# A hybrid decoder step on one core: the sample caches' compressed branch in single-pass matmuls, with its start-up loads and page table rearranged

## The chip, the cores and the metric

The kernel runs on 1 core of one Trainium2 chip. The metric is the device time of one execution in microseconds (us), the median of several runs. Engines are TensorE (PE; its weight loads are PEld), VectorE (DVE), ScalarE (ACT), GpSimd (POOL) and SyncE (SP, which here issues DMAs only).

## What is computed

One inference step of a decoder layer for a prompt of 512 tokens and 8 sample tokens, each sample with 1024 past positions in a paged cache. The change touches only the compressed branch of the samples' attention, and the code just before and behind it. From the reference:

```
def compress_kv(kv, pe, w1, b1, w2, b2):      # kv: cached K/V rows, 8 samples x 1024 positions
    ...
    seg = kv[:, :n_seg * CMP_STRIDE].reshape(B, n_seg, CMP_STRIDE, 2, N_KV, HEAD_DIM)
    w1r = w1.reshape(2, CMP_R, CMP_STRIDE, HEAD_DIM, CMP_HIDDEN)
    proj = jnp.einsum('bsjcgd,crjdf->bsrcgf', seg, w1r)
    hid = sum(proj[:, r:r + n_cmp, r] for r in range(CMP_R))
    pe_term = jnp.einsum('cld,cldf->cf', pe, w1)
    hid = jax.nn.silu(hid + (pe_term + b1)[None, None, :, None, :])
    return jnp.einsum('bncgf,cfd->bncgd', hid, w2) + b2[None, None, :, None, :]
```

Stride 16, blocks of 32, 4 KV heads of 64, hidden 128; c is K or V, r is the half of the block. A page of the cache holds 128 positions, and the page table says which page. Behind this come the norm of x, the input projection, the three attention branches, the SSD heads, the output projection and the MLP, all in float32 accuracy. Large products take three passes over operands split in a high part (type FP32R, written by ScalarE) and a low part (the rest, by VectorE): high x high, high x low, low x high.

## The kernel before

Each engine has one program, a list of functions called in order, and they meet through semaphores. Order of the functions at the start:

- SP: `const_sp`, `x_sp`, `proj_sp`. POOL: `const_pool`, `compress_pool`, `const2_pool`. ACT: `compress_act`, `x_act`, `proj_act`. DVE: `const_dve`, `compress_dve`, `x_dve`, `proj_dve`. PE: `const_pe`, `compress_pe`, `x_pe`, `proj_pe`.

**Start.** `const_sp` issues 12 loads of 128 single words (the page table, repeated onto 128 partitions), then 16 small loads, the last two (`dskip`) of 4-byte words, and after the first gather has landed the weights `w1` (2 MB). `const_dve` turns the table into row indices `idx_c` (4 steps of the branch) and `idx_s`. `compress_pool` gathers 4 MB of cache rows per step by an indirect DMA into the one buffer `seg_raw`; the gather of the next step waits until `seg_raw` has been reordered.

**The branch.** There are N_ST = 4 steps t of 2 samples. In each step DVE copies `seg_raw` into `seg_ord` in 8 pieces (L464, one for each c and KV head), PE turns each piece by 8 transposes of 128x128 into PSUM banks 0 to 3 (`turn`, L368), and ACT and DVE, half of the banks each, copy the turned data to `segT` (L424, L456). Then `products` (L382) does 32 matmuls of 128x512 in plain float32; the trace has each of these as two matmul records, so 64 records in a step. ACT evicts the second half r = 1, DVE adds r = 0 (L479), ACT applies SiLU, and `second_layer` (L390, L397) multiplies by `w2`. `outputs` on DVE (L446, L451) stores the results. PE's order is turn(0), the bias product L331 (64 matmul records with one column each, `w1` as weights), turn(1), products(0), turn(2), second_layer(0), products(1), and so on.

**Behind it.** `x_sp` loads x (4 MB, `xtok`) onto the place of `segT` when products(2) is done, and then `proj_sp` fills the ring `w_raw` of four 0.5 MB weight pieces. `x_pe` turns x, ACT and DVE split it into `h_hi` and `h_lo` (L502, L526), and `proj_act` and `proj_dve` split the weight pieces (`hi_piece` L591, `lo_piece` L597) for the three-pass products of `mul_piece` (L610), which also do the rest of the projections and the MLP.

Of the kernel before, what the change touches and what calls it, by code (L numbers as in the profile page):

```python
# [105 lines left out]
def build_program(nc, i, o):  # L106
    with ExitStack() as ctx:
# [69 lines left out]
        segT = at("segT", [P, 2, 8, 8, P], A2)  # L177
        w1 = at("w1", [P, 2, 2, 8, CHID], A2 + 65536)

        xtok = at("xtok", [P, 4, D_MODEL], A2)  # L180
        xs_tok = at("xs_tok", [NB, D_MODEL], M_LO)
# [22 lines left out]
        ptab_c = at("ptab_c", [P, 4], 11488, I32)  # L204
        ptab_s = at("ptab_s", [P, NB], 11520, I32)
# [26 lines left out]
        SMALL_LOADS.append((pe_row[:], i["cmp_pe"].rearrange("a c (l j) d -> (a c l) (j d)", j=2)))  # L232
# [9 lines left out]
        def const_sp(e):  # L242

            pg = i["page_table"]
            for s in range(4):
                e.dma_start(ptab_c[:, s:s + 1], bass.AP(pg.tensor, 16 * s, [[1, 16], [0, 8]]),
                            allow_slow_non_contiguous=True).then_inc(tab_ld, 16)
            for b in range(NB):
                e.dma_start(ptab_s[:, b:b + 1], bass.AP(pg.tensor, 8 * b, [[1, 8], [0, 16]]),
                            allow_slow_non_contiguous=True).then_inc(tab_ld, 16)  # L250
            e.wait_ge(pool_c, 1)
            for dst, src in SMALL_LOADS:
                e.dma_start(dst, src, allow_slow_non_contiguous=True).then_inc(small_ld, 16)
            e.wait_ge(seg_ld, 16)
            e.dma_start(w1[:].rearrange("p c r j f -> p c (r j) f"),
                        i["cmp_w1"].rearrange("a c (l j) d f -> (a j d) c l f", j=2)).then_inc(w1_ld, 16)

        def const_pool(e, ch):
# [5 lines left out]
            ch.step(e.iota(pidx[:, 0:1], pattern=[[0, 1]], base=0, channel_multiplier=1))  # L264
            ch.step(e.memset(ident[:], 0.0))
            keep(ident[:], ALU.not_equal, 1.0, 0, 1, [[-1, P]])
            ch.settle()
            e.memset(ones[:], 1.0).then_inc(pool_c, 1)

        def const2_pool(e, ch):  # L270
# [4 lines left out]
            for tile, v in ((cmask, 0.0), (causT, 1.0), (cmpmask, 0.0), (same_grp, 1.0), (sel_mat, 1.0),  # L275
                            (sel_m2, 1.0), (own_batch, 1.0), (valid0, 1.0), (small, 1.0), (eps_col, EPS)):
                ch.step(e.memset(tile[:], v))
# [19 lines left out]
        def const_dve(e, ch):  # L297
# [5 lines left out]
            e.wait_ge(tab_ld, 16 * 12)  # L303
            for s in range(4):
                e.scalar_tensor_tensor(out=idx_c[:, s:s + 1], in0=ptab_c[:, s:s + 1], scalar=8.0,
                                       in1=pidx[:, 1:2], op0=ALU.mult, op1=ALU.add).then_inc(idx_rdy, 1)
            for b in range(NB):
                e.scalar_tensor_tensor(out=idx_s[:, b:b + 1], in0=ptab_s[:, b:b + 1], scalar=16.0,
                                       in1=pidx[:, 2:3], op0=ALU.mult, op1=ALU.add).then_inc(idx_rdy, 1)

            e.wait_ge(pe_par, 2)
            ch.step(e.tensor_copy(pcol[:], PS[:, 0, 0:P]))
            e.tensor_copy(peT[:], PS[:, 1, 0:32]).then_inc(par_c, 1)
            ch.settle()

        def bias_dve(e):
            e.wait_ge(pe_par, 3)
            e.tensor_tensor(bias1[:], PS[:, 4, 0:2], pcol[:, R_B1:R_B1 + 2], ALU.add).then_inc(par_c, 1)

        def const_pe(e):  # L320
            e.wait_ge(pool_c, 2)
            e.wait_ge(small_ld, 16 * N_SMALL)
            e.transpose(PS[:, 0, 0:P], prow[:], ident[:]).then_inc(pe_par, 1)
            e.transpose(PS[:, 1, 0:32], pe_row[:], ident[0:32, 0:32]).then_inc(pe_par, 1)

        def bias_pe(e):

            e.wait_ge(w1_ld, 16)
# [8 lines left out]
        seg_ld, c_order = sem("seg_ld"), sem("c_order")  # L337
# [8 lines left out]
        def compress_pool(e):  # L346
            rows_c = i["cache_kv_cmp"].rearrange("a n (s j) c g d -> (a n s) (j c g d)", j=STRIDE)
            for t in range(N_ST):
                if t == 0:
                    e.wait_ge(idx_rdy, 4)  # L350
                else:
                    e.wait_ge(c_order, 8 * t)
# [4 lines left out]
        def compress_pe(e):  # L357
            e.wait_ge(par_c, 1)
            def turn(t):
                for cg in range(8):  # L360
                    e.wait_ge(c_order, 8 * t + cg + 1)
                    for h in range(2):
                        f = (t * 8 + cg) * 2 + h
                        if f >= 4:
                            e.wait_ge((c_ev_act, c_ev_dve)[h], f // 2 - 1)
                        for x in range(4):
                            j = 2 * (4 * h + x)
                            last = e.transpose(PS[:, f % 4, x * P:x * P + P],  # L368
                                               seg_ord[:, cg, j:j + 2, :].rearrange("p j d -> p (j d)"), ident[:])
                        last.then_inc(c_turned, 1)  # L370

            def products(t):
                e.wait_ge(c_ev_act, 8 * (t + 1))
                e.wait_ge(c_ev_dve, 8 * (t + 1))
                for r in (1, 0):
                    for c in range(2):
                        if t and r == 1:
                            e.wait_ge(c_half, 2 * t)
                        elif t:
                            e.wait_ge((c_kout, c_vout)[c], t)  # L380
                        for j in range(8):
                            last = e.matmul(PS[:, 4 + 2 * c + r, :], w1[:, c, r, j, :],  # L382
                                            segT[:, t % 2, 4 * c:4 * c + 4, j, :],
                                            start=(j == 0), stop=(j == 7))
                        last.then_inc(c_prod, 1)
# [15 lines left out]
            turn(0)  # L401
            bias_pe(e)
            for t in range(N_ST):
                if t + 1 < N_ST:
                    turn(t + 1)
                if t == 0:
                    e.wait_ge(par_c, 2)
                if t:
                    second_layer(t - 1)
                products(t)  # L410
            second_layer(N_ST - 1)

        def turned_copy(t, h, copy, done, e):

            if t >= 2:
                e.wait_ge(c_prod, 4 * (t - 1))
            for cg in range(8):
                f = (t * 8 + cg) * 2 + h
                e.wait_ge(c_turned, f + 1)
                copy(segT[:, t % 2, cg, 4 * h:4 * h + 4, :],  # L420
                     PS[:, f % 4, :].rearrange("p (j s) -> p j s", j=4)).then_inc(done, 1)

        def compress_act(e):
            copy = lambda out, in_: e.activation(out, in_, ACT.Copy)  # L424
            turned_copy(0, 0, copy, c_ev_act, e)
            for t in range(N_ST):
                if t + 1 < N_ST:
                    turned_copy(t + 1, 0, copy, c_ev_act, e)
                for c in range(2):
                    e.wait_ge(c_prod, 4 * t + c + 1)  # L430
                    if t:
                        e.wait_ge(c_sum, 2 * t)
                    copy(second[:, c].rearrange("p g n -> p (g n)"), PS[:, 5 + 2 * c, :]).then_inc(c_half, 1)
                e.wait_ge(par_c, 2)
                for c in range(2):
                    e.wait_ge(c_sum, 2 * t + c + 1)
                    if t:
                        e.wait_ge(c_w2, 2 * t)
                    e.activation(hid_s[:, c, :, 0:NCMP_S], hid[:, c, :, 0:NCMP_S], ACT.Silu,
                                 bias=bias1[:, c:c + 1]).then_inc(c_silu, 1)  # L440

        def compress_dve(e):
# [13 lines left out]
            copy = lambda out, in_: e.tensor_copy(out, in_)  # L456

            def order(t):

                e.wait_ge(seg_ld, 16 * (t + 1))  # L460
                for cg in range(8):
                    if t:
                        e.wait_ge(c_turned, 16 * (t - 1) + 2 * cg + 2)
                    e.tensor_copy(seg_ord[:, cg], seg_raw[:, :, cg, :]).then_inc(c_order, 1)  # L464
            order(0)
            turned_copy(0, 1, copy, c_ev_dve, e)
            bias_dve(e)
            for t in range(N_ST):
                if t + 1 < N_ST:
                    order(t + 1)  # L470
                    turned_copy(t + 1, 1, copy, c_ev_dve, e)
                if t:
                    outputs(t - 1)
                for c in range(2):
                    e.wait_ge(c_prod, 4 * t + 3 + c)
                    e.wait_ge(c_half, 2 * t + 1 + c)
                    if t:
                        e.wait_ge(c_silu, 2 * t)
                    e.tensor_tensor(hid[:, c, :, 0:NCMP_S],  # L479
                                    PS[:, 4 + 2 * c, :].rearrange("p (g n) -> p g n", n=64)[:, :, 0:NCMP_S],  # L480
                                    second[:, c, :, 1:64], ALU.add).then_inc(c_sum, 1)
# [9 lines left out]
        def x_sp(e):  # L491
            e.wait_ge(c_prod, 4 * (N_ST - 1))
            for t in range(4):
                e.dma_start(xtok[:, t, :], i["x_prompt"][0, t * P:t * P + P, :]).then_inc(xs_ld[t], 16)
            e.dma_start(xs_tok[:], i["x_sample"].rearrange("b t d -> (b t) d")).then_inc(xs_ld[4], 16)

        def x_act(e, ch):
            e.wait_ge(pool_c, 3)
# [2006 lines left out]
```

## Time and profile before

| | us |
|---|---|
| median of 3 runs | 2975.57 (2968.17 to 2980.98) |
| the profiled execution | 2988.49 |
| its span in the trace | 2986.8 |
| mean granted TensorE clock, share of full | 0.961 |

The profile is of one execution. A busy time is the time in which an engine had an instruction of that kind; the chain is the list of work, followed back from the last instruction, in which each piece waited for the one before it. Only what stands on the chain, or would stand there if something else got shorter, counts for the time. In the span of 2986.8 us the branch of this change ends at 213 us.

### The profile page before, as it was taken

The page shows a single profiled execution, that of the slowest core. Times are in us where ns is not written, and L with a number is a line of the kernel's source. Part 1 is how long each engine was busy: PE and PEld are TensorE (multiplying, and loading weights), DVE is VectorE, ACT ScalarE, POOL GpSimd, SP SyncE. Part 2 cuts the span into 40 slices and gives each one's busy share as a digit, 9 for nine tenths or more (in the row PEclk, how much of TensorE's full clock was granted, in tenths as well). Part 3 has the DMA queues.
Part 4 walks back from the last instruction along what each step waited for, and adds up shares of the span by engine and source line. Part 5 has one row for each costly group of instructions (what it writes and reads, how often), then busy time and mean ns, then how long its engine had stood idle before and what let it go on. Part 6 is the DMA issues. An engine that isn't in the chain of part 4 may idle for free.

```text
span 2986.8 us, 51003 instructions
## 1 busy us (share of the span) xinstructions
PE 2820.8 (94%) x21260; PEld 2613.5 (88%) x21260; DVE 1122.8 (38%) x1659; ACT 803.9 (27%) x1277; POOL 103.9 (3%) x115
## 2 busy tenths in 40 slices
PE   4899999996899978989999999999999999999998
PEld 4449999996788635689899999999999999999998
DVE  2322222225588266454333233333333333333333
ACT  1213111114254123443222221222212222122233
POOL 0000000000000002201100000000000000000001
PEclk9999999998699988799999999999999999999999
DMA  5135333332001852322222222222222222222222
GB/s 185 71 114 169 92 91 91 91 86 79 2 1 43 263 204 79 96 95 93 85 86 91 92 91 91 92 91 91 91 91 91 91 91 91 91 91 91 92 91 85
DMA packets 251881, 287.16 MB, mean 96 GB/s; under 512 B 21549, under 2 KB 244139, under 8 KB 247814
## 3 DMA queue, kind: packets, MB, share of 16 engines
q1 hardware_dynamic: 249214, 239.99, 25.7%
q0 software_dynamic: 2592, 46.14, 4.0%
q8 instruction: 51, 0.84, 0.1%
q14 instruction: 24, 0.20, 0.0%
HBM read 273.68 MB, written 20.71 MB: 99 GB/s over the span
## 4 chain that ended last, share of the span: by engine, by line
PE 90%; DVE 4%; DMA 3%; ACT 2%; issue 1%; SPq 0%; POOL 0%; ACTq 0%; POOLq 0%; DVEq 0%
PE PS L610 70%; PE PS L382 4%; PE PS L1112 2%; PE PS L1100 1%; DMA win_t<-kvs_tok 1%; PE PS L1081 1%; PE PS L1878 1%; DMA sel_t<-in_cache_kv_sel,idx_s 1%; PE PS L1365 1%; PE PS L368 1%; PE PS L1832 1%; PE PS L1082 1%; DMA seg_raw<-in_cache_kv_cmp,idx_c 1%; PE PS L1329 1%; DVE seg_ord L464 1%
## 5 line engine op out<-in xcount | busy, mean ns | idle before, releaser
L597 DVE TENSOR_TENSOR w_lo<-w_raw,w_hi 128x1024 fp32r<-128x1024 f32 (+1 forms) x388 | 460.3, 1190 | 1378.6 <-ACT w_hi L591 1377.6
L591 ACT ACTIVATE w_hi<-w_raw 128x1024 fp32r<-128x1024 f32 (+1 forms) x388 | 395.6, 1024 | 1502.1 <-PE PS L610 1502.0
L610 PE MATMUL PS<-h_hi,w_hi 128*128 128x260 f32 x3360 | 675.3, 282 | 7.4 <-DVE w_lo L597 5.1
L610 PE MATMUL PS<-h_lo,w_hi 128*128 128x260 f32 x3360 | 675.2, 282 | 0.0
L610 PE MATMUL PS<-h_hi,w_lo 128*128 128x260 f32 x3360 | 673.9, 282 | 0.0
L610 PEld LDWEIGHTS PS<-h_hi,w_hi 128*128 128x128 f32 x3360 | 516.4, 189 | 8.2 <-issue 7.5
L610 PEld LDWEIGHTS PS<-h_lo,w_hi 128*128 128x128 f32 x3360 | 519.2, 189 | 0.0
L610 PEld LDWEIGHTS PS<-h_hi,w_lo 128*128 128x128 f32 x3360 | 518.1, 189 | 0.0
L610 PE MATMUL PS<-u_hi,w_hi 128*128 128x260 f32 x2048 | 411.3, 282 | 8.4 <-DVE u_lo L2279 8.4
L610 PE MATMUL PS<-u_lo,w_hi 128*128 128x260 f32 x2048 | 410.6, 282 | 0.0
L610 PE MATMUL PS<-u_hi,w_lo 128*128 128x260 f32 x2048 | 410.0, 281 | 0.0
L610 PEld LDWEIGHTS PS<-u_hi,w_hi 128*128 128x128 f32 x2048 | 313.7, 188 | 10.1 <-issue 10.1
L610 PEld LDWEIGHTS PS<-u_lo,w_hi 128*128 128x128 f32 x2048 | 315.5, 188 | 0.0
L610 PEld LDWEIGHTS PS<-u_hi,w_lo 128*128 128x128 f32 x2048 | 314.8, 188 | 0.0
L382 PE MATMUL PS<-segT,w 128*128 128x512 f32 x256 | 110.8, 593 | 0.0
L610 PE MATMUL PS<-mix_hi,w_hi 128*128 128x260 f32 x512 | 103.6, 284 | 7.5 <-DVE w_lo L597 7.5
L610 PE MATMUL PS<-mix_lo,w_hi 128*128 128x260 f32 x512 | 103.5, 284 | 0.0
L610 PE MATMUL PS<-mix_hi,w_lo 128*128 128x260 f32 x512 | 103.2, 283 | 0.0
L382 PEld LDWEIGHTS PS<-segT,w 128*128 128x128 f32 x256 | 48.3, 190 | 59.5 <-issue 59.3
L2169 DVE TENSOR_TENSOR x_acc<-PS,x_acc 128x520 f32 (+1 forms) x144 | 93.5, 691 | 11.2 <-PE PS L610 11.2
L1138 ACT ACTIVATE prob<-PS,negmax 128x128 f32<-128x128 f32 (+3 forms) x128 | 65.8, 526 | 79.1 <-DVE negmax L1156 79.1
L610 PEld LDWEIGHTS PS<-mix_hi,w_hi 128*128 128x128 f32 x512 | 79.3, 190 | 7.6 <-issue 7.6
(394 smaller groups left out, 2463.0 us busy)
## 6 DMA issues: line engine op xcount, KB each, us to landing
w_raw<-in_w_up SPq DMA_DIRECT2D x256, 256.0 KB, 2.8
w_raw<-in_w_down SPq DMA_DIRECT2D x256, 256.0 KB, 2.8
w_raw<-in_w_in SPq DMA_DIRECT2D x160, 256.0 KB, 2.9
w_raw<-in_w_out SPq DMA_DIRECT2D x64, 256.0 KB, 3.0
out_kv_win_s<-in_state_kv_win SPq DMA_DIRECT2D x8, 1022.0 KB, 7.7
win_t<-in_state_kv_win SPq DMA_DIRECT2D x16, 448.0 KB
xtok<-in_x_prompt SPq DMA_DIRECT2D x4, 1024.0 KB, 9.1
x_r<-in_x_prompt SPq DMA_DIRECT2D x4, 1024.0 KB, 6.3
```

The source lines that it names most:

```text
L368: last = e.transpose(PS[:, f % 4, x * P:x * P + P], seg_ord[:, cg, j:j + 2, :].rearrange("p j d -> p (j d)"), ident[:])
L382: last = e.matmul(PS[:, 4 + 2 * c + r, :], w1[:, c, r, j, :], segT[:, t % 2, 4 * c:4 * c + 4, j, :], start=(j == 0), stop=(j == 7))
L464: e.tensor_copy(seg_ord[:, cg], seg_raw[:, :, cg, :]).then_inc(c_order, 1)
L591: ins = e.activation(hi, raw, ACT.Copy)
L597: ins = e.tensor_tensor(lo, raw, hi.bitcast(F32), ALU.subtract)
L610: mm = e.matmul(PS[:, bank + 2 * m + h, 0:HN], w, x[:, k0 + k, h * HN:h * HN + HN], start=st and c == 0, stop=sp and c == 2)
L1081: e.matmul(PS[:, qt, 0:w], q, k_hh[b][g][:, 0:w], start=True, stop=False)
L1082: e.matmul(PS[:, qt, 0:w], q, k_ll[b][g][:, 0:w], start=False, stop=False)
L1100: last = e.transpose(PS[:, 4 + n, c0 + (qt - kt) * P:c0 + (qt - kt) * P + P], prob[:, u % 2, c:c + P], ident[:])
L1112: last = e.matmul(PS[:, 7, kt * P:SEQ], kv_tok[:, kt, c:c + P], probT(u, kt), start=(b == 0 and kt == 0), stop=False)
L1138: e.activation(prob[:, u % 2, P_OFF[qt]:P_OFF[qt] + w], PS[:, qt, 0:w], ACT.Exp, bias=negmax[:, u % 2, qt:qt + 1], accum_out=den[:, u % 2, ...
L2169: e.tensor_tensor(x_acc[:, tile], PS[:, bank:bank + 2, 0:HN], x_acc[:, tile], ALU.add).then_inc(g_out, 1)
```

## The change

1. The page table is loaded once as two small tiles (16 x 4 and 8 x 8 words). GpSimd makes a one-hot matrix `sel_pg` (which partition belongs to which table row), PE multiplies, and DVE forms the indices from PSUM. `pe_row` is loaded third.
2. `w1` is loaded first of all, from ACT's queue (`const_act`), and the bias product moves ahead of the branch, before all turns.
3. `w1` and the turned cache rows are split into high and low parts, and the products take three single-pass FP32R matmuls in place of one float32 matmul (384 matmuls of 128x512 in all).
4. A step is cut into two units u (c = 0, c = 1), 8 in all, each turned in two lots of 4 banks: turn(u+1, 0), products(u, 1), turn(u+1, 1), products(u, 0). All high parts are ACT's, all low parts DVE's. DVE reorders both units of the next step in one go (`seg_order`), ahead of `outputs`.
5. `x_sp` starts x when products(6) are done, and the sample rows and `proj_sp` when products(7) are. The splits of the first two weight pieces move into the loops of `x_act` (behind k = 11 and 13) and `x_dve` (behind k = 12 and 14).

```
-            for s in range(4):
-                e.dma_start(ptab_c[:, s:s + 1], bass.AP(pg.tensor, 16 * s, [[1, 16], [0, 8]]), ...
-            for b in range(NB):
-                e.dma_start(ptab_s[:, b:b + 1], bass.AP(pg.tensor, 8 * b, [[1, 8], [0, 16]]), ...
+            e.dma_start(ptab_c[:], bass.AP(pg.tensor, 0, [[1, 16], [16, 4]]), ...
+            e.dma_start(ptab_s[:], bass.AP(pg.tensor, 0, [[1, NB], [NB, NB]]), ...
+            e.dma_start(pe_row[:], i["cmp_pe"].rearrange("a c (l j) d -> (a c l) (j d)", j=2)).then_inc(tab_ld, 16)
...
-            e.wait_ge(seg_ld, 16)
+
+        def const_act(e):
             e.dma_start(w1[:].rearrange("p c r j f -> p c (r j) f"),
...
+            ch.step(e.memset(sel_pg[:], 1.0))
+            for x, w in enumerate((8, 16)):
+                keep(sel_pg[:, x, :], ALU.is_ge, 0.0, 0, -w, [[1, P]])
+                keep(sel_pg[:, x, :], ALU.is_ge, 0.0, w - 1, w, [[-1, P]])
...
+            e.tensor_copy(page_c[:], ptab_c[:]).then_inc(par_c, 1)
+            e.tensor_copy(page_s[:], ptab_s[:]).then_inc(par_c, 1)
+            e.wait_ge(pe_par, 1)
+            ch.settle()
+            e.scalar_tensor_tensor(out=idx_c[:], in0=PS[:, 2, 0:4], scalar=8.0,
+                                   in1=p_mod[:, 0:1].to_broadcast([P, 4]), op0=ALU.mult, op1=ALU.add).then_inc(idx_rdy, 1)
...
         def const_pe(e):
             e.wait_ge(pool_c, 2)
+            e.wait_ge(par_c, 2)
+            e.matmul(PS[:, 2, 0:4], sel_pg[:, 0, :], page_c[:], start=True, stop=True)
+            e.matmul(PS[:, 2, 4:12], sel_pg[0:NB, 1, :], page_s[:], start=True, stop=True).then_inc(pe_par, 1)
+            e.wait_ge(pool_c, 3)
+            e.wait_ge(tab_ld, 16 * 3)
+            e.transpose(PS[:, 1, 0:32], pe_row[:], ident[0:32, 0:32]).then_inc(pe_par, 1)
+            bias_pe(e)
             e.wait_ge(small_ld, 16 * N_SMALL)
             e.transpose(PS[:, 0, 0:P], prow[:], ident[:]).then_inc(pe_par, 1)
...
+            def products(u, r):
+                c = u % 2
+                for j in range(8):
+                    hi, lo = seg_hi[c][:, :, j, :], seg_lo[c][:, :, j, :]
+                    wh, wl = w1_hi[:, c, r, j, :], w1_lo[:, c, r, j, :]
+                    for n, (w, x) in enumerate(((wh, hi), (wh, lo), (wl, hi))):
+                        last = e.matmul(PS[:, 4 + 2 * c + r, :], w, x, start=(j + n == 0), stop=(j + n == 9))
+                last.then_inc(c_prod, 1)
...
+            e.wait_ge(par_c, 4)
+            turn(0, 0)
+            turn(0, 1)
+            e.wait_ge(w1_split[0], 4)
+            e.wait_ge(w1_split[1], 4)
+            for u in range(2 * N_ST):
+                t, c = divmod(u, 2)
+                if u + 1 < 2 * N_ST:
+                    turn(u + 1, 0)
+                e.wait_ge(c_ev_dve, 8 * (u + 1))
                 if t:
+                    e.wait_ge(c_half, u - 1)
+                products(u, 1)
+                if u + 1 < 2 * N_ST:
+                    turn(u + 1, 1)
+                if t and c == 0:
                     second_layer(t - 1)
+                if t:
+                    e.wait_ge((c_kout, c_vout)[c], t)
+                products(u, 0)
...
+            e.wait_ge(pe_par, 3)
+            for c in range(2):
+                for r in range(2):
+                    e.wait_ge(w1_split[0], 2 * c + r + 1)
+                    e.tensor_tensor(w1_lo[:, c, r], w1[:, c, r], w1_hi[:, c, r].bitcast(F32),
+                                    ALU.subtract).then_inc(w1_split[1], 1)
+            bias_dve(e, ch)
+            seg_order(e, 0)
+            seg_order(e, 1)
+            seg_low(e, 0)
+            for u in range(2 * N_ST):
+                t, c = divmod(u, 2)
+                if u + 1 < 2 * N_ST:
+                    seg_low(e, u + 1)
+                if c == 0 and t + 1 < N_ST:
+                    seg_order(e, u + 2)
+                    seg_order(e, u + 3)
+                if t and c == 0:
+                    outputs(t - 1)
+                e.wait_ge(c_prod, 2 * u + 2)
+                e.wait_ge(c_half, u + 1)
...
         def x_sp(e):
-            e.wait_ge(c_prod, 4 * (N_ST - 1))
+            e.wait_ge(c_prod, 2 * (2 * N_ST - 1))
             for t in range(4):
                 e.dma_start(xtok[:, t, :], i["x_prompt"][0, t * P:t * P + P, :]).then_inc(xs_ld[t], 16)
+            e.wait_ge(c_prod, 4 * N_ST)
             e.dma_start(xs_tok[:], i["x_sample"].rearrange("b t d -> (b t) d")).then_inc(xs_ld[4], 16)
```

## Rows read from the trace of the kernel before

**Rows 1.** The page: the chain by line, and two groups of instructions.

```profile
PE PS L610 70%; PE PS L382 4%; PE PS L1112 2%; PE PS L1100 1%; DMA win_t<-kvs_tok 1%; PE PS L1081 1%; PE PS L1878 1%; DMA sel_t<-in_cache_kv_sel,idx_s 1%; PE PS L1365 1%; PE PS L368 1%; PE PS L1832 1%; PE PS L1082 1%; DMA seg_raw<-in_cache_kv_cmp,idx_c 1%; PE PS L1329 1%; DVE seg_ord L464 1%
...
L597 DVE TENSOR_TENSOR w_lo<-w_raw,w_hi 128x1024 fp32r<-128x1024 f32 (+1 forms) x388 | 460.3, 1190 | 1378.6 <-ACT w_hi L591 1377.6
L591 ACT ACTIVATE w_hi<-w_raw 128x1024 fp32r<-128x1024 f32 (+1 forms) x388 | 395.6, 1024 | 1502.1 <-PE PS L610 1502.0
```

**Rows 2.** Busy time by stretch: stretch, length, engines' busy us, clock, DMA share, GB/s.

```profile
0.00:71.00 71.00, 31.23 (x195) 30.21 (x196) 21.49 (x48) 10.65 (x17) 4.26 (x12) 0.90 0.48 172
71.00:213.00 142.00, 131.73 (x481) 67.64 (x480) 31.26 (x53) 21.55 (x34) 5.80 (x27) 1.00 0.29 108
```

**Rows 3.** The timeline of the first 61 us: start, duration, what.

```profile
0.82 2.62 SPq L246 DMA_DIRECT2D ptab_c<-in_page_table  x4
...
3.48 5.19 SPq L249 DMA_DIRECT2D ptab_s<-in_page_table  x8
...
14.41 1.36 SPq L253 DMA_DIRECT2D dskip<-in_d_skip  x2
17.41 0.37 DVE L305 SCALAR_TENSOR_TENSOR idx_c<-ptab_c,pidx 128x1 uint32<-128x1 int32 x4 [15.12 <-DMA ptab_s<-in_page_table]
...
28.43 0.45 PE L323 MATMUL PS<-ident,prow 128*128 128x128 f32 x1 [28.43 <-DMA dskip<-in_d_skip]
...
48.96 11.35 PE L331 MATMUL PS<-peT,w 128*128 128x1 f32 x64
```

**Rows 4.** DMA issues of the first 330 us: size, median us to landing.

```profile
seg_raw<-in_cache_kv_cmp,idx_c POOLq DMA_INDIRECT x4, 15.1
...
w<-in_cmp_w SPq DMA_DIRECT2D x1, 0.5 KB, 10.0
```

**Rows 5.** The chain in order of time: start, duration, what.

```profile
18.07 19.88 DMA seg_raw<-in_cache_kv_cmp,idx_c
...
60.42 4.91 DVE seg_ord L464 x8
...
71.01 27.48 PE PS L382 x64
...
104.67 5.02 PE PS L368 x44
109.69 0.58 PE PS L390 x8
110.27 0.91 PE PS L397 x16
...
181.86 27.68 PE PS L382 x64
...
230.92 25.34 PE PS L610 x192
258.13 446.01 PE PS L610 x3744
```

**Rows 6.** A group of instructions of the first 330 us: busy, mean ns.

```profile
L456 DVE COPY segT<-PS 128x512 f32<-128x512 f32 x32 | 21.7, 690 | 4.7 <-PE PS L368 4.7
```

**Rows 7.** Three stretches by engine; the column behind POOL's is the granted clock.

```profile
52.00:54.00 2.00, 2.00 (x11) 2.00 (x11) 0.00 (x0) 0.00 (x0) 0.00 (x0) 0.50 1.19 500
62.00:64.00 2.00, 2.00 (x12) 2.00 (x10) 2.00 (x4) 0.60 (x1) 0.00 (x0) 0.50 0.00 0
68.00:70.00 2.00, 2.00 (x21) 2.00 (x20) 1.62 (x3) 1.45 (x3) 0.00 (x0) 1.00 0.66 279
```

**Rows 8.** The loads of x: time from issue to landing.

```profile
DMA to landing us min/median/max: 4.9/9.1/13.1
```

**Rows 9.** The timeline where x is turned and the projection starts.

```profile
213.00 0.63 PE L549 MATMUL PS<-ident,xtok 128*128 128x128 f32 x4 [0.82 <-issue]
...
229.48 1.29 DVE L597 TENSOR_TENSOR w_lo<-w_raw,w_hi 128x512 fp32r<-128x512 f32 x2 [2.16 <-ACT w_hi L591]
```

More of the change, by code:

```diff
@@ L267, in const_pool @@
             ch.settle()
-            e.memset(ones[:], 1.0).then_inc(pool_c, 1)
+            e.memset(eps_col[:], EPS).then_inc(pool_c, 1)
         def const2_pool(e, ch):
@@ L357, in compress_pe, with turn @@
         def compress_pe(e):
[L358 to L361, printed above, removed]
+            def turn(u, half):
+                t, c = divmod(u, 2)
+                for g in (2 * half, 2 * half + 1):
+                    e.wait_ge(c_order, u * NKV + g + 1)
                     for h in range(2):
-                        f = (t * 8 + cg) * 2 + h
+                        f = (u * NKV + g) * 2 + h
                         if f >= 4:
-                            e.wait_ge((c_ev_act, c_ev_dve)[h], f // 2 - 1)
+                            e.wait_ge(c_ev_dve, f - 3)
                         for x in range(4):
@@ L368, in turn @@
                             last = e.transpose(PS[:, f % 4, x * P:x * P + P],
-                                               seg_ord[:, cg, j:j + 2, :].rearrange("p j d -> p (j d)"), ident[:])
+                                               seg_ord[:, c * NKV + g, j:j + 2, :].rearrange("p j d -> p (j d)"),
+                                               ident[:])
                         last.then_inc(c_turned, 1)
[L372 to L385, printed above, removed]
+            def products(u, r):
[6 more added lines that the diff above has]
+                last.then_inc(c_prod, 1)
             def second_layer(t):
@@ L423, in compress_act @@
-        def compress_act(e):
[L424 to L440, printed above, removed]
@@ new lines, in seg_low @@
+        def seg_low(e, u):
+            for g in range(NKV):
+                for h in range(2):
+                    f = (u * NKV + g) * 2 + h
+                    e.wait_ge(c_ev_act, f + 1)
+                    e.tensor_tensor(seg_lo[u % 2][:, g, 4 * h:4 * h + 4, :],
+                                    PS[:, f % 4, :].rearrange("p (j s) -> p j s", j=4),
+                                    seg_hi[u % 2][:, g, 4 * h:4 * h + 4, :].bitcast(F32),
+                                    ALU.subtract).then_inc(c_ev_dve, 1)
@@ L467, in compress_dve @@
[L467 to L471, printed above, removed]
-                if t:
[L473 to L481, printed above, removed]
+            e.wait_ge(pe_par, 3)
@@ new lines, in compress_dve @@
+            for c in range(2):
+                for r in range(2):
+                    e.wait_ge(w1_split[0], 2 * c + r + 1)
[5 more added lines that the diff above has]
+            seg_low(e, 0)
+            for u in range(2 * N_ST):
+                t, c = divmod(u, 2)
+                if u + 1 < 2 * N_ST:
+                    seg_low(e, u + 1)
[6 more added lines that the diff above has]
+                e.wait_ge(c_half, u + 1)
+                if t:
+                    e.wait_ge(c_silu, u - 1)
+                e.tensor_tensor(hid[:, c, :, 0:NCMP_S],
+                                PS[:, 4 + 2 * c, :].rearrange("p (g n) -> p g n", n=64)[:, :, 0:NCMP_S],
+                                second[:, c, :, 1:64], ALU.add).then_inc(c_sum, 1)
```

127 lines of the change are left out of this document (74 added, 53 removed).

## The prediction, on record before the result

> **What bounds the kernel now.** I read the page first: its chain is 70% the three-pass products of L610, which the change does not touch, and only 4% the branch's products L382 [rows 1]. So the change can only act in the stretch before the projection, and I cut that in two. In the first 71 us PE is busy for 31 us; in the next 142 us for 132 us [rows 2]. The reader should see two different limits: a start that waits for transfers, and a branch that waits for PE.
>
> The start by the timeline [rows 3]: the last of the 12 page-table loads is issued at 8.7 us (3.48 + 5.19) and the first index is formed at 17.41, released by that load. The small loads end with `dskip` at 28.4. The chain [rows 5] has the first gather from 18.07 for 19.88 us, so it lands at 37.95. Then come the turns, the bias product (11.35 us from 48.96 [rows 3]), a second reordering of 4.91 us at 60.42, more turns, and the first products at 71.01. In the branch a step's 64 product records take 27.48 us [rows 5], 430 ns each. Each record streams 512 columns twice, since at full clock 512 columns take 213 ns at 2.4 GHz; a step is thus 128 passes of 215 ns. The last products end at 209.5 (181.86 + 27.68), and x is first turned at 213.0 [rows 9].
>
> **The start, part by part.**
> *Page table.* Twelve loads of 128 words took 16.6 us (from 0.82 to the release at 17.41 [rows 3]), 1.4 us each. Three loads of 64, 64 and 32 pieces would be in by about 5 us; if they share the engines with `w1` they could be held until `w1` is in. I take 6. The one-hot matrix on GpSimd (one memset, four selects) runs beside this. Two copies, two tiny matmuls and the index form a chain of short instructions that the trace does not show together; I give it 2 us (bounds 1 and 4). The gather starts at 8 (bounds 7 to 13) in place of 18.07 and lands 19.88 later [rows 5], at 28. The median gather takes 15.1 [rows 4], but the first one had the longer time on an almost idle DMA, so I keep it.
> The Trainium skill (DMA: Bandwidth & Descriptors, Anatomy of one DMA) has a fixed cost of about 2.0 us for a transfer; by it the three loads would land at about 4.4 us, and the sum would be 1.6 us better than with my 6. The 1.4 us per load in the row is a rate of loads in a row and does not test it.
> *w1.* It is issued at about 0.8 and takes 10.0 us [rows 4] (the row `w<-in_cmp_w` with a landing time), so it is in at 11. Then on PE the bias product, 11.35 us [rows 3], at half clock as it was from 52 us on [rows 7]: to 22. VectorE may overwrite `w1` only then: four pieces at 1.19 us [rows 1] to 27, while ScalarE's four at 1.02 are long done. pcol and bias1 follow: the small loads, which ended with `dskip` 11 to 13 us after its issue, are in by about 20, so VectorE is free at 28. Both chains thus meet at 28.
> *First unit.* VectorE reorders two units, 8 x 0.61 = 4.9 us (4.91 [rows 5]), and only then does the low parts of unit 0, 8 x 0.69 = 5.5 (a copy of the same size out of PSUM takes 0.69 [rows 6]). The second lot of turns waits for them, and the first lot of unit 1 as well; adding a fill and its eviction, 12 us. The products start at 40 (36 to 46), 31 us earlier than before. What goes: the bias product and the second full turn no longer stand between the gather and the products.
>
> **The branch, from the first product to x** (142 us before).
> - Products: 384 passes. Bounds: 215 ns, as a pass in L382 costs; or 235 ns, the time per column of L610 (446.01 us / 3744 = 119 ns for 260 columns [rows 5]). I take 216, as the width of 512 is that of L382: 83 us, 27 less than 110 (90 at the upper bound). The Trainium skill (TensorE: Matmul & The Clock Gate, the section on 56 ns against 53.3 ns) has a gap of N/2.4 + 2.5 ns, 215.7 at 512 columns; its 110.8 at 260 is below the 119 of the row, so it does not settle the case of split operands. By it the sum would be the same.
> - Turns: a lot has 16 transposes at 114 ns (5.02 / 44 [rows 5]), 1.9 us; 13 of the 16 lots come after the first product: 25 us.
> - Second layers: three at 1.5 us (0.58 + 0.91 [rows 5]) and the last with its waits, 3.5 us (209.5 to 213.0): 8 us.
> - A new wait. In units 2 and 4 VectorE does, after the low parts, eight reorderings (4.9 us) and then `outputs`, for which PE waits before products(u, 0), as they write the same bank. After the second lot is turned VectorE needs 2.0 us for the remaining low parts, 4.9, and 0.6 for the keys' output; PE has 1.5 us of second layer in that time. So PE stalls 6.0 us twice, and 1.1 in unit 6, which has no reordering: 13 us. Queued behind `outputs` on VectorE is hid(u), which itself waits for the products.
> - Clock: transposes sparse as at 62 to 64 ran at half clock, and dense ones at 68 to 70 at full clock, with only transposes between [rows 7]. The first products may run at half clock for 3 to 4 us: 1.7 (0 to 5).
> The sum is 83 + 25 + 8 + 13 + 1.7 = 131, 11 less than 142. Gathers are hidden: each is issued when the pair before it is reordered (at about 33, 55 and 84), takes 15.1 [rows 4], and is wanted over 15 us later.
> - x: four loads issued behind products(6), at 157; the slowest landed 13.1 us after issue [rows 8], so about 171. Products(7) and the last second layer end at 171 too. Before, 30 us of products covered this load; now about 14 do, and the sample rows come only behind products(7). I add 0.5, and up to 6 in the range. x is turned from 171.3, not 213.0: 41.7 us gained.
>
> **Behind it.** Before, `lo_piece` 0 ends at 230.8 and PE starts at 230.92 [rows 5, 9]. VectorE's x work ended at 227.3 (229.48 less 2.16 idle). Two pieces of 1.29 within it make it 229.9, so PE starts 0.9 earlier, relative to x. The gap on PE shrinks to under 2 us, and the first block, 192 records in 25.34 us, would take 22.9 at 119 ns: up to 2.5 more. The first weight piece is issued only at 168, but is wanted at about 181. I take 3.0 together (0 to 3.4). Nothing later changes: ScalarE and VectorE have slack there, 1502 and 1379 us idle [rows 1].
>
> **Sum.** 31 + 10.7 + 3 = 44.7 us. The profiled execution took 2988.5 (span 2986.8), so it would be 2943.8; that execution lies 12.9 above the median 2975.6, from which the same saving gives 2931. A change of under 0.5% (15 us) can't be told from none in this kernel, as its three runs spread over 13.
>
> **Rivals.**
> 1. *The clock stays at half in the branch.* Turns in lots between groups of products, with stalls of 6 us on PE: at half clock a pass is 427 ns and 384 of them cost 81 us more, 208 transposes at 213 instead of 114 another 21, less the 13 of stalls that vanish: +89, so 3020, slower than before. It decides once about 210 of the 384 passes are slow. The half clock at 52 to 54 under one-column matmuls speaks for it; the clock of 1.00 over 71 to 213, with 10 us of idle PE in it, against [rows 2, 7]. Chance 0.03. The Trainium skill says for this (TensorE: Matmul & The Clock Gate, Part 4) that transposes do not count as busy for the clock; the rise between 62 and 70 with only transposes on PE disagrees.
> 2. *A 512-column FP32R pass costs what a float32 record did, 430 ns.* 384 x 0.214 = +82, so 3013. L610's 119 ns for 260 columns speaks against. Chance 0.03.
> 3. *Hand-offs eat the branch's gain.* VectorE has 4.9 + 11.0 + 1.4 + 1.3 = 18.6 us in a step against PE's 31; if every lot waits for its low parts (two hand-offs of 1.5 us a unit, 24 us), the branch is longer than before, and 20 us remain: 2955. Against: a lot's low parts take 2.8 us beneath 5.2 of products. Chance 0.12.
> 4. *The start gains little*, because gather, table and `w1` share the DMA engines or the gather starts late, and x lies open by 6 us: products from 60, and 2957 to 2965. Chance 0.07.
> 5. *Almost no stalls, full clock, a gather of 15 us*: 13 + 2 + 4, so 2912. Chance 0.07.
> The forecast has 0.68.
>
> **How the numbers follow.** The forecast's own range, from the bounds of its terms (start +6/-4, products +7, stalls +5/-10, clock +3, x +6, tail +3), is 2920 to 2948. The range reaches from 2915, into rival 5, to 2956, over rival 3: it leaves out rivals 1, 2, most of 4 and part of 5, under 0.2. Faster by over 0.5% (below 2961): the forecast, rivals 3 and 5, and a third of 4, 0.89. Within 0.5%: 0.05. Slower: rivals 1 and 2, 0.06.
>
> **What the profile of the changed kernel would show.** First gather issued near 8 us and landing near 28; the first reordering at 28; the first product at 40 at half clock. Products at 216 ns a pass, L610-like three in a row. PE waiting for `kc_T`'s output in units 2 and 4, some 6 us each. The first turned x at 171. L610 from about 188, in place of 230.9, at full clock. The prediction is wrong if the gather lands after 35, if a pass costs over 235 ns, if the clock is at half after 50 us, or if PE waits more than 5 us for x.

## The result, and the profile after

The changed kernel took 2945.59 us (median of 4 runs, 2935.11 to 2953.16), the kernel before 2978.28 (4 runs). The ratio is 0.9873 with a 95% interval of 0.9845 to 0.9901. In a later comparison on another occasion, 6 runs against 11, it was 0.9886 (0.9852 to 0.9920). So the change makes the kernel faster by 1.1 to 1.3%, or 34 to 38 us. The forecast was 2931 with a range of 2915 to 2956, and a chance of 0.89 for faster by over 0.5%.

The page of the changed kernel; L403 is the products, L392 the turns, L666 the three-pass products.

```profile
span 2938.7 us, 51338 instructions
PE 2799.8 (95%) x21392; PEld 2640.0 (90%) x21392; DVE 1144.3 (39%) x1688; ACT 820.5 (28%) x1314; POOL 104.9 (4%) x120
PE PS L666 71%; PE PS L403 3%; PE PS L1172 2%; PE PS L1160 1%; DVE c_tmp L1715 1%; PE PS L392 1%; PE PS L1141 1%; DMA sel_t<-in_cache_kv_sel,idx_s 1%; PE PS L1938 1%; PE PS L1142 1%; PE PS L1389 1%; PE PS L1955 1%; PE PS L1892 1%; PE PS L1399 1%; DVE seg_ord L459 0%
```

The two profiles differ by 48 us of span, but not all of that is the change. The chain of the changed kernel, in order of time (start, duration, what), shows where it leaves the branch:

```profile
0.87 11.37 DMA w<-in_cmp_w
12.24 0.14 issue
12.38 13.80 PE PS L354 x64
26.18 0.02 issue
26.20 4.63 DVE w_lo L511 x4
30.83 0.21 DVE pcol L332
...
31.23 4.81 DVE seg_ord L459 x8
...
42.74 5.48 PE PS L403 x24
48.22 1.75 PE PS L392 x16
49.97 5.46 PE PS L403 x24
...
80.62 4.90 DVE seg_ord L459 x8
85.52 0.52 DVE kc_T L497 x2
86.04 0.04 issue
86.09 7.23 PE PS L403 x24
...
123.94 7.05 PE PS L403 x24
...
194.09 25.12 PE PS L666 x192
...
221.08 38.98 PE PS L666 x325
```

The reader should compare the last row with 258.13 in [rows 5]: the projection's second block starts 37.05 us earlier. The first product stands at 42.7 and not at 71.0. The first 31 us of the chain are now `w1`, the bias product and the split; the gather is not on it. In units 2 and 4 a reordering and `kc_T`'s output stand ahead of the products.

The other 11 us of span lie far behind, where the pages of the selected and window branches are gathered. In this stage `sel_t` and `win_t` are loaded, and `mix_lo` stands at its end. It went from chain rows as these in the changed kernel

```profile
956.97 10.37 DMA sel_t<-in_cache_kv_sel,idx_s
...
994.80 13.03 DMA sel_t<-in_cache_kv_sel,idx_s
...
1239.73 2.53 DVE mix_lo L2179 x4
```

to these in a second profile of the same kernel:

```profile
958.42 10.81 DMA sel_t<-in_cache_kv_sel,idx_s
1059.69 21.55 DMA win_t<-kvs_tok
1233.99 2.53 DVE mix_lo L2179 x4
```

From the first turned x to `mix_lo` it took 1075.6 us in the profile before, 1062.7 in the first after and 1056.1 in the second, and 1059 to 1075 in the first eight experiments, none of which touches its gathers. This stage varies from run to run by more than 10 us. The two profiles with the old order lie at its high end (1075.6, and 1071.6 in experiment 8), but the ratios stand for 34 to 38 us in all, so they leave no sign of a gain there. So I judge each kernel by its marks before 260 us, and by the ratio only where several runs were timed. The marks repeat to about 1.2 us: the two profiles of the changed kernel have the first product at 42.7 and 41.5, the first turned x at 177.0 and 177.9, and the second block at 221.1 and 222.3.

### The profile page after: what moved, and what is told of

The parts are those of the page before. It is cut to its first block, busy times and chain, and to the rows that moved or that the text cites. A ratio compares the mean times of both kernels' runs of the same rounds, so it can differ in the third digit from the quotient of the medians.

```text
span 2938.7 us, 51338 instructions
## 1 busy us (share of the span) xinstructions
PE 2799.8 (95%) x21392; PEld 2640.0 (90%) x21392; DVE 1144.3 (39%) x1688; ACT 820.5 (28%) x1314; POOL 104.9 (4%) x120
## 4 chain that ended last, share of the span: by engine, by line
PE 89%; DVE 6%; ACT 2%; issue 1%; DMA 1%; POOL 0%; ACTq 0%; POOLq 0%; DVEq 0%
PE PS L666 71%; PE PS L403 3%; PE PS L1172 2%; PE PS L1160 1%; DVE c_tmp L1715 1%; PE PS L392 1%; PE PS L1141 1%; DMA sel_t<-in_cache_kv_sel,idx_s 1%; PE PS L1938 1%; PE PS L1142 1%; PE PS L1389 1%; PE PS L1955 1%; PE PS L1892 1%; PE PS L1399 1%; DVE seg_ord L459 0%
## 5 line engine op out<-in xcount | busy, mean ns | idle before, releaser
L647 ACT ACTIVATE w_hi<-w_raw 128x1024 fp32r<-128x1024 f32 (+1 forms) x388 | 395.6, 1024 | 1502.2 <-PE PS L666 1501.9
L666 PE MATMUL PS<-h_hi,w_hi 128*128 128x260 f32 x3360 | 676.3, 283 | 5.9 <-DVE h_lo L580 3.6
L666 PE MATMUL PS<-h_lo,w_hi 128*128 128x260 f32 x3360 | 675.9, 283 | 0.0
L666 PE MATMUL PS<-h_hi,w_lo 128*128 128x260 f32 x3360 | 674.8, 282 | 0.0
L666 PEld LDWEIGHTS PS<-h_hi,w_hi 128*128 128x128 f32 x3360 | 517.0, 189 | 6.8 <-DVE h_lo L580 3.7
L666 PEld LDWEIGHTS PS<-h_lo,w_hi 128*128 128x128 f32 x3360 | 519.6, 189 | 0.0
L666 PEld LDWEIGHTS PS<-h_hi,w_lo 128*128 128x128 f32 x3360 | 518.5, 189 | 0.0
L666 PE MATMUL PS<-u_hi,w_hi 128*128 128x260 f32 x2048 | 411.8, 282 | 8.4 <-DVE u_lo L2339 8.4
L666 PE MATMUL PS<-u_lo,w_hi 128*128 128x260 f32 x2048 | 411.1, 282 | 0.0
L666 PE MATMUL PS<-u_hi,w_lo 128*128 128x260 f32 x2048 | 410.5, 282 | 0.0
L666 PEld LDWEIGHTS PS<-u_hi,w_hi 128*128 128x128 f32 x2048 | 313.8, 188 | 10.0 <-issue 10.0
L666 PEld LDWEIGHTS PS<-u_lo,w_hi 128*128 128x128 f32 x2048 | 315.5, 189 | 0.0
L666 PEld LDWEIGHTS PS<-u_hi,w_lo 128*128 128x128 f32 x2048 | 314.9, 188 | 0.0
L666 PE MATMUL PS<-mix_hi,w_hi 128*128 128x260 f32 x512 | 104.0, 285 | 7.5 <-DVE w_lo L653 7.5
L666 PE MATMUL PS<-mix_lo,w_hi 128*128 128x260 f32 x512 | 103.9, 285 | 0.0
L666 PE MATMUL PS<-mix_hi,w_lo 128*128 128x260 f32 x512 | 103.5, 284 | 0.0
L666 PEld LDWEIGHTS PS<-mix_hi,w_hi 128*128 128x128 f32 x512 | 79.6, 191 | 7.6 <-issue 7.6
L666 PEld LDWEIGHTS PS<-mix_lo,w_hi 128*128 128x128 f32 x512 | 80.1, 191 | 0.0
L666 PEld LDWEIGHTS PS<-mix_hi,w_lo 128*128 128x128 f32 x512 | 79.8, 191 | 0.0
```

Of the source, the lines that this page charges most:

```text
L647: ins = e.activation(hi, raw, ACT.Copy)
L666: mm = e.matmul(PS[:, bank + 2 * m + h, 0:HN], w, x[:, k0 + k, h * HN:h * HN + HN], start=st and c == 0, stop=sp and c == 2)
```

## The experiments

Marks are: the first reordering, the first product, the first turned x, and the start of the projection's second block (PE after the row-norm gap). The changed kernel has 31.1, 42.7, 177.0 and 221.1. One execution each, except for the last four. The single executions took, in the order of experiments 1 to 4, 2929.5, 2960.1, 2965.3 and 2965.3 us, beside 2988.9 for one of the kernel before on the same chip, and in the order of 5 to 8, 2934.5, 2940.4, 2935.1 and 2979.4, beside 2984.9.

**1. Outputs first.**

```
                     seg_low(e, u + 1)
+                if t and c == 0:
+                    outputs(t - 1)
                 if c == 0 and t + 1 < N_ST:
                     seg_order(e, u + 2)
                     seg_order(e, u + 3)
-                if t and c == 0:
-                    outputs(t - 1)
```

> VectorE's outputs go ahead of its eight reorderings in units 2 and 4; nothing else changes. Theory (the reorderings are what PE waits for): the changed kernel turns x first at 177.0 us; the two stalls of 5.7 us before products(2, 0) and products(4, 0) shrink to about 1, as in unit 6, and those two groups of 24 products, which took 7.23 and 7.05 us in place of 5.46 at a clock that had fallen, take 5.5 again. x is turned at about 164 (13 us earlier). Rival (the wait only moves): the reorderings come later, the next lot of turns waits for them, and x is turned at 172 or later.

x was turned at 164.3, 12.7 us earlier. The theory holds: of each wait of 5.73 us before the products of units 2 and 4 there are 0.92 left. This is the chain of that kernel:

```profile
71.33 5.49 PE PS L403 x24
...
80.98 5.75 PE PS L403 x24
88.48 5.46 PE PS L403 x24
...
112.54 5.76 PE PS L403 x24
...
144.12 16.65 PE PS L403 x72
```

The groups behind the former stalls begin at 80.98 (86.09 before this edit) and take 5.75 us, not 7.23. The stretches of the changed kernel say why (stretch, length, engines' busy us, granted clock, DMA share, GB/s):

```profile
79.00:86.00 7.00, 1.35 (x24) 1.21 (x20) 7.00 (x14) 1.14 (x3) 0.21 (x1) 0.74 0.01 2
86.00:89.00 3.00, 2.91 (x7) 2.34 (x8) 0.62 (x2) 0.00 (x0) 2.64 (x14) 0.50 0.61 175
89.00:94.00 5.00, 5.00 (x27) 4.14 (x26) 0.65 (x1) 0.00 (x0) 2.92 (x12) 0.98 0.97 419
```

PE is busy for 1.35 of 7 us, its clock falls to half (0.50 from 86 to 89), and the first products behind the stall run at 1.2 GHz. VectorE is busy all of those 7 us. A stall of 5.7 us thus cost 7.5. With the outputs first the clock stays at full:

```profile
78.00:84.00 6.00, 5.08 (x43) 4.27 (x41) 6.00 (x12) 1.85 (x4) 0.00 (x0) 1.00 0.01 3
```

**2. Plain float32 products in the new order.**

```
-                    for n, (w, x) in enumerate(((wh, hi), (wh, lo), (wl, hi))):
-                        last = e.matmul(PS[:, 4 + 2 * c + r, :], w, x, start=(j + n == 0), stop=(j + n == 9))
+                    last = e.matmul(PS[:, 4 + 2 * c + r, :], w1_hi[:, c, r, j, :].bitcast(F32),
+                                    seg_hi[c][:, :, j, :].bitcast(F32), start=(j == 0), stop=(j == 7))
```

> The changed kernel with one float32 matmul for each three single-pass ones; it leaves out the low parts in the products, but still makes them. Theory (a float32 matmul of 512 columns costs 860 ns, as before the change, and three single passes 683, by 5.46 us for 24): a group of 8 takes 6.88 us instead of 5.46, 16 groups add 22.7 us, and x is turned at about 199 to 200. Rival (the branch goes at the pace of its hand-offs and the products' price hides beneath it): x is turned within 8 us of 177.0.

x was turned at 201.3, 24.3 us later. A group took 6.87 us in the chain of that kernel, the price before the change (27.48 / 4), and the one behind the stall 9.80:

```profile
42.33 6.87 PE PS L400 x16
50.94 6.87 PE PS L400 x16
...
92.63 9.80 PE PS L400 x16
```

1.4 us in 16 groups are 22.5; the rest is the slower clock behind the two stalls, which costs 2.9 and 2.8 us here and 1.8 and 1.6 in the changed kernel. The single passes are worth this much, and nothing hides it.

**3. w1 late.** The load of `w1` goes from ACT's start back to SyncE's, behind `e.wait_ge(seg_ld, 16)`.

> The changed kernel with w1 issued by SyncE after the first gather has landed, as before the change. Theory (the early load is what carries the start): w1 lands some 10 us after the gather (gather at about 21, w1 at 31), the bias product of 13.8 us ends at 45, VectorE's split at 50, the first product stands at about 61 in place of 42.7, and x is turned at about 195. Rival (the gather sets the start): the first product moves by under 5 us.

The first product stood at 67.3 (24.6 later) and x at 203.7. The chain:

```profile
5.42 15.91 DMA seg_raw<-in_cache_kv_cmp,idx_c
21.42 15.63 DMA w<-in_cmp_w
...
67.30 5.47 PE PS L402 x24
```

The theory holds in kind, but both marks came later than forecast, as `w1` took 15.6 us in place of 10. From 21 to 25 us nothing of it moved (DMA share 0.03 to 0.05), with the word loads of `dskip` in flight, which had been issued ahead of it on the same queue; experiment 8 tests such loads ahead of the gather. The early load carries the start of the changed kernel.

**4. Page table as before.** Twelve loads of 128 words and indices formed straight from them, in place of the one-hot product.

> The changed kernel with the page table loaded by 12 transfers of 128 words and no one-hot product, as before the change. Theory (in the changed kernel the chain w1, bias product, split and not the gather sets the start, so that much of the one-hot product's gain is slack): the first gather is issued near 18 and lands at 33 to 36 instead of near 22, while VectorE is free at about 31, or later if peT, behind the same loads, comes too late for the bias product (18 + 13.8 + 5, so 37). The first product moves by 2 to 7 us. Rival (the gather is what counts): it moves by all of the 11 us by which the gather is later.

The first product stood at 53.8 (11.0 later) and x at 189.5. The rival named the 11 us, but for another reason. The gather was issued at 22.7 and landed at 42.3:

```profile
22.73 19.53 DMA seg_raw<-in_cache_kv_cmp,idx_c
...
53.77 5.49 PE PS L399 x24
```

That is 20 us later than in the changed kernel, where it landed at 22.2 and the first reordering waited until 31.2. The theory's slack of 9 us is there, and the 11 us are what exceeds it. Two things made the gather later than I expected. The indices were formed at 22.1 and not at 17.4: the last table load was issued at 12.2, beside `w1`'s transfer, and not at 8.7, and the indices here also wait for `pe_row`, the thirteenth load, which landed at 22.0. And the gather itself took 19.5 us and not the 14.9 of the changed kernel, as `dskip` had been issued just ahead of it. So this edit costs 11 us, but how much of that is the table alone is not shown: a part belongs to the wait for `pe_row` and to `dskip`'s place ahead of the gather.

**5. Weight pieces split behind the x loops again.** The four lines with `k in (11, 13)` and `k in (12, 14)` go, and `proj_act` and `proj_dve` split all pieces.

> The changed kernel with the splits of the first two weight pieces back behind the x loops. From the first turned x (177.0 us) to the first product of the projection took 17.9 us before the change and 17.1 in the changed kernel. Theory (0.8 us is all that the move brings, since its gap on PE of 3.6 us still lets the clock fall): 17.9 again, the projection's first product at 194.9, and the second block 0.8 to 1.0 us later than 221.1. Rival (the first pieces now come late behind x and the move covers more than that): over 19 us.

x at 176.9, first projection product at 194.86, second block at 221.68. From x to the first projection product it is 17.9 us, as in the kernels before and of experiment 8; all kernels here with the pieces moved, but for the last of experiment 9, have 17.1. So the move is worth 0.8 us there. The 0.6 us at the second block lie within the scatter of that mark. In the changed kernel's timeline PE still waits 3.6 us, and its matmuls run at 217 ns, two in 0.43:

```profile
194.09 0.80 PE L666 MATMUL PS<-h_hi,w_hi 128*128 128x260 f32 x2 [3.60 <-DVE h_lo L580]
194.69 0.64 PE L666 MATMUL PS<-h_lo,w_hi 128*128 128x260 f32 x2
195.12 0.64 PE L666 MATMUL PS<-h_hi,w_lo 128*128 128x260 f32 x2
```

**6. Contiguous columns.** `seg_hi` and `seg_lo` are laid out `[P, 8, 4, P]`, so that a product streams one run of 512.

> The changed kernel with the turned rows stored so that a product's 512 columns are one contiguous run in place of four runs of 128; ScalarE and VectorE write them in four strided runs. A group of 24 single-pass products takes 5.46 us, 227.6 ns each, where 215 or 216 was reckoned. Theory (the 12 ns are a cost of each single-pass matmul with its own split weights, as L610 shows 11 ns over its columns' time at 260): still 5.46 us, x turned at 177. Rival (the runs cost it): 5.2 us or less, x turned at 173 or before.

Groups took 5.46 to 5.50 us and x was turned at 176.9. The layout costs nothing, and what a pass takes over the forecast's 216 ns is not a matter of how its columns lie.

**7. Reordering before the split.** VectorE's first rows of `compress_dve`:

```
+            seg_order(e, 0)
+            seg_order(e, 1)
             e.wait_ge(pe_par, 3)
...
-            bias_dve(e, ch)
-            seg_order(e, 0)
-            seg_order(e, 1)
             seg_low(e, 0)
+            bias_dve(e, ch)
```

PE turns unit 0 before it transposes `prow`, into bank 6.

> The changed kernel with VectorE's first two reorderings ahead of the split of w1, the turns of unit 0 ahead of the small parameters' transpose (which moves to bank 6), and pcol and bias1 behind the low parts of unit 0. In the changed kernel the first gather lands near 22 and the first reordering stands at 31.15, behind bias product (to 26.2), split and pcol. Theory (VectorE's order is what keeps the landed rows waiting): reordering at 22, split from 27 to 31.5, low parts from 31.5 to 38, first product at 38.3 in place of 42.7, x turned at 172.6. Rival (PE's half clock and the turns set the pace, not VectorE): under 2 us earlier.

The first product stood at 37.9, 4.8 us earlier, and x at 173.7, only 3.3 earlier. The groups behind the two stalls took 8.23 and 7.63 us this time:

```profile
37.91 5.49 PE PS L402 x24
...
81.26 8.23 PE PS L402 x24
...
120.12 7.63 PE PS L402 x24
```

In the second profile of the changed kernel they took 8.59 and 7.78, and in the first 7.23 and 7.05. So what the clock costs behind the same stall differs by 1.4 us between two executions of one kernel; what decides it was not tried.

**8. The kernel before, with `dskip` loaded behind `w1`.**

> The kernel before, with the two loads of d_skip (1024 single words) issued behind w1 and not ahead of the first gather. Before, the gather was issued at 18.07 and landed after 19.88 us; data moved only from 24 us on, while word loads were in flight; the next gathers took 14 to 15. Theory (word loads in flight hold back the gather's data): it lands after 14 to 16 us, at 33, the bias product still waits for turn(0), and x is turned 4 to 5 us before 213.0. Rival (the first gather is slow by itself): it lands after 19 to 20 us again, and x is turned within 1 us of 213.0.

The first gather took 13.4 us, x was turned at 207.3, 5.7 us before 213.0. The chain, and the stretch behind the gather's issue, of this kernel:

```profile
18.08 13.39 DMA seg_raw<-in_cache_kv_cmp,idx_c
...
31.56 4.92 DVE seg_ord L466 x8
```

```profile
18.00:24.00 6.00, 0.69 (x2) 0.36 (x2) 0.80 (x7) 0.00 (x0) 1.19 (x1) 1.00 0.72 262
```

The same stretch of the kernel before:

```profile
18.00:24.00 6.00, 0.00 (x0) 0.00 (x0) 0.40 (x5) 0.00 (x0) 1.19 (x1) 1.00 0.04 0
```

With the word loads ahead of it, nothing of the gather moved until 24 us. The theory holds; x gains 1 us more than forecast.

**9. Four kernels on one chip, 6 runs each against 11 of the kernel before.**

> The changed kernel once more, beside the three improved ones and the kernel before on one chip. x turned at 177.0 us, second block at 221.1, against 213.0 and 258.1 before: 37 us, 1.24%. Theory (what the profile shows gained until 221 us is all that is gained; the other 11 us of the profiles' difference come from the gathers of the selected and window branches, whose stage varied by 16 us among the kernels so far): ratio 0.9875 within 0.001. Rival (the later stage gains too): 0.984.

> Outputs first and the first reorderings before the split, together. Outputs first gave 12.7 us and the start 4.8 at the first product, of which 1.5 was lost again to slower products behind the stalls. Theory (with the stalls gone nothing is lost again): first product at 37.9, x turned at 159.7, ratio to before 0.9820. Rival (the parts overlap): x turned at 162 or later.

> As the one before, and only the quarter of w1 that the first products need is split ahead of the low parts of unit 0; the other three quarters (3.5 us of VectorE) follow in the first unit. Theory (VectorE sets the start): first product 3.5 us earlier, at 34.5, x turned at 156.5. Rival (the gather lands at 22, PE at half clock turns four fills in 3.6 us, and the moved pieces delay the low parts of unit 1): under 1.5 us, x turned at 158.3 or later.

> As the one before, with the first two weight pieces split at k = 7 to 10 of the x loops in place of 11 to 14. In the changed kernel PE idled 3.6 us before the projection and its first 20 products took 217 ns each. Theory (the gap gets short enough to keep the clock): the gap is under 3 us, the first block of 192 takes 23.1 us in place of 25.1, 2 to 3 us in all. Rival (the pieces have not landed so early and ScalarE waits in the loop): later than the one before.

| kernel | first product | x turned | second block | ratio to before (95%) |
|---|---|---|---|---|
| changed, again | 41.5 | 177.9 | 222.3 | 0.9886 (0.9852 to 0.9920) |
| outputs first + reordering first | 38.0 | 159.8 | 204.7 | 0.9843 (0.9807 to 0.9880) |
| + split in stages | 34.0 | 156.6 | 201.4 | 0.9828 (0.9792 to 0.9863) |
| + pieces at k = 7 to 10 | 34.0 | 156.7 | 201.8 | 0.9854 (0.9825 to 0.9883) |

The changed kernel's ratio agrees with its 37 us (0.9875). The two orders together give what their parts gave, and a little more: the waits are down to 0.9 us, the groups behind them take 5.74 us, and little is lost to the clock. Their marks are as forecast; their ratio came out at 0.9843, with an interval that holds the forecast 0.9820. The staged split gives 3.2 us more, as forecast:

```profile
33.97 5.48 PE PS L402 x24
...
173.75 25.80 PE PS L676 x192
201.42 58.59 PE PS L676 x490
```

Splitting the pieces still earlier gives nothing. PE's last wait for `h_lo` fell to 1.6 us, but the loop has more short waits, and the projection started at 174.77 in place of 173.75. The clock fell within the loop (0.50 from 170 us on): four turns of x, 0.66 us at full clock, took 1.1, and the first block, still at half clock at its start, took 25.2 us and not the 23.1 of the theory. The rival's time came true, but ScalarE was not seen waiting for the pieces.

The staged kernel lies 56.7 us before the kernel before at the second block (258.1 less 201.4); its ratio stands for 51 us, with an interval of 41 to 62. Its lead over the two orders alone shows in the marks and not in the ratios. The last kernel's marks say 56.3 us, a ratio of 0.9811, and its interval leaves that out. In the profiles of these three the stage from x to `mix_lo` took 1070 to 1072 us, against 1056 to 1065 in eight of the other nine with the new order. So a part of what is gained before 260 us may be lost in the later gathers; this was not tried.

## Why the prediction was right

The likeliest case came true, at the lower part of its gain: 37 us of 44.7. By its own terms:

| term | forecast | measured |
|---|---|---|
| first product, against 71.0 | 40 | 42.7 |
| products at full clock | 83 | 87.5 (16 x 5.47) |
| turns, 13 lots | 25 | 22.8 (13 x 1.75) |
| second layers and the end | 8 | 8.2 (the rest) |
| stalls before products | 13 | 12.4 |
| slow clock in the branch | 1.7 | 3.4 |
| branch, first product to x | 131 | 134.3 |
| x open | 0.5 | 0 |
| behind x | 3.0 | 1.0 |
| gain | 44.7 | 37.0 |

The steps held: the bias product and the second turn left the way between gather and products, the new stall of VectorE's order stood where it was put (units 2, 4, and a small one in 6), and rival 1 (half clock through the branch) and rival 2 (430 ns a pass) did not come. One sign that the prediction set against itself did come in part: the clock was at half after 50 us, behind the two stalls and again at the start of the projection. What was mis-sized:

- *The start, 2.7 us.* The chain of `w1`, bias product and split is the one that bounds, and it was 3.2 us longer than forecast; the first unit behind it took 11.5 and not 12. `w1` landed at 12.24, not 11, and the bias product took 13.80 us, not 11.35. In the kernel before, the 64 matmuls follow each other at 112 ns until 51.4 us, as they began at full clock at the end of the turns, and at 213 ns after; here, with PE coming from idle, all are 213 ns apart, though PE is busy throughout. (The profile's clock column reads 1.00 here, but these distances are those of half clock.) The gather's part was wrong too, without a price: three loads were in by 5.4 us (forecast 6; the 4.4 beside it was too short), and the gather took 14.9 us, not 19.88, so it landed at 22.2 and not at 28, long before it was needed. I kept the long time as a property of the first gather; experiment 8 shows that it belonged to the word loads ahead of it. That both chains would meet at 28 was thus wrong for both.
- *The pass, 4.5 us.* I took 216 ns because the width is that of L382, and 235 as the bound; it is 227.6 (5.46 / 24). L610's 260 columns take 119. At half clock, 1.2 GHz, those 260 columns took 217 ns, one for each cycle; by that, 512 take 213 at full clock and 260 take 108. Both single-pass rows lie 11 to 14 ns over their columns' time at 2.4 GHz, the two-pass record of L382 only 3 over (430 less 427). The nearer row was that with the same kind of operand, not that with the same width. The sentence on the 2.5 ns of the Trainium skill (TensorE: Matmul & The Clock Gate, the section on 56 ns against 53.3 ns) went with the value taken, and neither single-pass row bears it out.
- *The clock, 1.7 us more, at another place.* The first products ran at full clock (5.48 for 24); the slow ones stand behind the two stalls, where I priced only the wait.
- *Behind x, 2.0 us.* The move of the pieces gives 0.8 us; the 2.5 us for the clock did not come. I had PE's gap under 2 us. It was 5.12 before and is 3.60, as PE's last turns came 0.7 us later behind the first turned x than before, and the projection's first product 0.8 earlier. The first 20 products still ran at half clock.
- *The turns*, 109 ns and not 114 each, gave back 2.2 us.
- *x* was not open: its four loads landed within 10.9 us of issue, and the first turn waited for `vc`.

One sum in the working does not hold. The 2920 to 2948 of the forecast's own range do not follow from the bounds beside it: added up they give 2917 to 2961, and as the root of their squares 2920 to 2944. The measured 2945.6 lies inside 2920 to 2948 and 2917 to 2961, and just outside 2920 to 2944. The four larger errors all went the same way, for which bounds taken as independent leave no room.

Rival 3 was wrong, as ScalarE and VectorE keep up with the lots, but its concern was right in one place: VectorE's order. The parts' worths do not add: undoing the single passes costs 24 us, `w1` first 27, the one-hot table 12.5, 63 together against 37. The stalls of the new order take 16 back (12.4 and 3.4). For the other 10 I have an argument and no run: the page table and `w1` each are worth their time only while the other is early, and experiments 3 and 4 also pay for `dskip`'s place.

## What to carry to other kernels

An engine that serves two waiters should serve the one on the critical path first: moving two small outputs ahead of eight copies gave a third of what the whole change gave. Price a stall of PE with what the clock loses behind it, here 1.6 to 3.2 us on top of 5.7. For the cost of a matmul take the row with the same kind of operand and correct it for the width; and keep loads of single words out of the way of the first large transfer.

## What the runs showed of the hardware

- Loads of 4-byte words in flight held back large transfers issued behind them. The first gather of 4 MB, on GpSimd's queue, took 19.9 and 19.5 us with `dskip`'s 1024 words issued just ahead on SyncE's. In the first of these the DMA share stood at 0.04, with no bandwidth, for 6 us. It took 13.4 us with the words much later, and 14.9 to 15.9 with them issued up to 2 us behind it. `w1`, issued at 21.4 behind such loads on their own queue, took 15.6 us in place of 10.0. What in the DMA path does this was not tried.
- A single-pass FP32R matmul of 512 columns, each with its own weights, takes 227.6 ns at full clock, whether its columns lie in one run or in four.
- Transposes alone raise the clock: in the kernel before it rose from 0.50 at 62 to 64 us to 1.00 at 68 to 70 with nothing but float32 transposes on PE ([rows 7]). This goes against the Trainium skill (TensorE: Matmul & The Clock Gate, Part 4: PE-mode transpose), whose times there are for bf16 ones.
- In the changed kernel PE was busy for 13.8 us with the 64 one-column matmuls of the bias product, and they stayed at the pace of half clock, 213 ns, from the first to the last; in the kernel before the clock fell from full to half under the same matmuls.
